# Expert stage of a two-block model: products from whole fp32 weights, one load for each expert, and blocks of 32, 64 and 128 rows in column tiles

## The reference, cut to what matters

```python
def hier_moe(h, w_group, b_group, w_expert, b_expert, w_gate, w_up, w_down):
    ...
    combine = jnp.sum(jax.nn.one_hot(global_i, N_EXPERTS, dtype=F32) * top_w[..., None], axis=1)
    out = jnp.zeros(hf.shape, F32)
    for e in range(N_EXPERTS):
        hid = jax.nn.silu(t @ w_gate[e]) * (t @ w_up[e])
        out = out + combine[:, e:e + 1] * (hid @ w_down[e]).astype(F32)
    return out.reshape(bsz, seq, d).astype(h.dtype)
```

## Time and profile before

| | us |
|---|---|
| median of 3 runs | 1953.18 |
| lowest and highest run | 1952.9 and 1956.12 |
| profiled execution, from its first to its last instruction | 1951.2 |
| first expert load issued, from the start of the span | 1359.78 |
| window 1555 to 1895: bytes moved | 415 GB/s |

### The profile page before, as it was taken

One profiled execution on the slowest core, in us unless ns is written; L12 is line 12 of the kernel. 1 busy time (PEld: TensorE's weight loads), 2 busy tenths in 40 slices (PEclk: granted clock), 3 DMA queues, 4 the chain that ended last, 5 costly groups with the idle time before them and its releaser, 6 DMA issues.

```text
span 1951.2 us, 23763 instructions
## 1 busy us (share of the span) xinstructions
PE 1847.8 (95%) x8321; PEld 1337.0 (69%) x8321; DVE 1412.4 (72%) x2128; ACT 1031.8 (53%) x1598; POOL 105.6 (5%) x98
## 2 busy tenths in 40 slices
PE   7999999999999899999999988887899999999998
PEld 6887777777888777777864545554688766556664
DVE  5988555455598855555756976434999999999995
ACT  5644555544564455554523112212888878777773
POOL 1000000000000000000003202000020100000001
PEclk9999999999999999999999999998999999999998
DMA  7544444345654444435545523231999999999994
GB/s 238 173 141 139 139 123 120 108 130 173 176 163 151 129 145 117 130 118 154 170 126 156 162 86 119 86 107 59 366 381 379 378 417 419 411 409 413 419 415 191
DMA packets 134437, 411.53 MB, mean 211 GB/s; under 512 B 16219, under 2 KB 18011, under 8 KB 107440
## 3 DMA queue, kind: packets, MB, share of 16 engines
q1 hardware_dynamic: 129200, 405.47, 59.1%
q0 software_dynamic: 5120, 4.56, 0.8%
HBM read 406.55 MB, written 12.39 MB: 215 GB/s over the span
## 4 chain that ended last, share of the span: by engine, by line
PE 64%; DVE 21%; DMA 6%; ACT 5%; issue 3%; SPq 0%; DVEq 0%; POOL 0%; ACTq 0%; POOLq 0%
PE bank L724 13%; PE bank L726 13%; PE bank L725 13%; PE bank L775 8%; DMA w_raw<-in_w_down 6%; DVE w_lo L1283 5%; PE bank L1208 3%; DVE r L1283 2%; DVE r L1289 2%; PE bank L851 2%; PE bank L692 2%; DVE y_lo L1283 2%; DVE h_lo L1283 1%; PE bank L1218 1%; PE bank L1219 1%
## 5 line engine op out<-in xcount | busy, mean ns | idle before, releaser
L1283 DVE TENSOR_TENSOR w_lo<-w_raw,w_hi 128x1024 fp32r<-128x1024 f32 x344 | 413.2, 1217 | 242.4 <-ACT w_hi L2293 223.4
L2293 ACT CAST w_hi<-w_raw 128x1024 fp32r<-128x1024 f32 x266 | 277.4, 1047 | 164.1 <-PE bank L726 157.0
L724 PE MATMUL bank<-w_hi,h_hi 128*128 128x512 f32 x800 | 327.5, 409 | 14.7 <-DVE w_lo L1283 14.7
L726 PE MATMUL bank<-w_hi,h_lo 128*128 128x512 f32 x800 | 315.4, 394 | 0.0
L725 PE MATMUL bank<-w_lo,h_hi 128*128 128x512 f32 x800 | 315.2, 394 | 0.0
L724 PEld LDWEIGHTS bank<-w_hi,h_hi 128*128 128x128 f32 x800 | 152.4, 190 | 51.2 <-issue 15.5
L726 PEld LDWEIGHTS bank<-w_hi,h_lo 128*128 128x128 f32 x800 | 152.3, 190 | 33.8
L2464 ACT ACTIVATE r<-bank,small 128x256 f32<-128x256 f32 (+1 forms) x152 | 63.9, 425 | 206.5 <-DVE small L1286 206.5
L725 PEld LDWEIGHTS bank<-w_lo,h_hi 128*128 128x128 f32 x800 | 152.9, 191 | 29.1
L775 PE MATMUL bank<-w_raw,h_all 128*128 128x512 f32 (+1 forms) x320 | 142.0, 600 | 1.1 <-DVE h_all L1283 1.1
L1283 DVE TENSOR_TENSOR w_lo<-r,w_hi 128x1024 fp32r<-128x1024 f32 x106 | 125.1, 1217 | 0.4 <-ACT w_hi L2590 0.4
(11 more groups left out here) (431 smaller groups left out, 3487.5 us busy)
## 6 DMA issues: line engine op xcount, KB each, us to landing
w_raw<-in_w_in SPq DMA_DIRECT2D x236, 512.0 KB, 3.7
r<-in_w_gate SPq DMA_DIRECT2D x70, 1024.0 KB, 7.2
w_raw<-in_w_down SPq DMA_DIRECT2D x70, 1024.0 KB, 7.8
r<-in_w_up SPq DMA_DIRECT2D x35, 1024.0 KB, 9.2
w_raw<-in_w_up SPq DMA_DIRECT2D x35, 1024.0 KB, 8.9
w_raw<-in_w_proj SPq DMA_DIRECT2D x48, 512.0 KB, 3.7
w_raw<-in_w_out SPq DMA_DIRECT2D x24, 512.0 KB, 4.0
w_raw<-in_w_mem_kv SPq DMA_DIRECT2D x8, 512.0 KB, 4.0
```

Source lines behind the costliest of these rows:

```text
L724: e.matmul(out_, sh, mh, start=first, stop=False, skip_group_check=shared)
L726: return e.matmul(out_, sl, mh, start=False, stop=last, skip_group_check=shared)
L1283: o.did(v.tensor_tensor(out_, a, b, op), sem, value)
L2293: a.copy(halves(n)[0], raw_of(n)).then_inc(w_hi, 1)
```

## The change

All of it is in the expert stage.

- **Loads.** Each expert is loaded once: 192 loads of 1 MiB instead of 210. There are 15 places of 1 MiB (`PLACES`: R7 to R10, the `w_hi/w_lo` buffers, the `h` and `y` buffers and `w_raw`). SP issues them in one plain order; load q waits until load q - 15's last use has been counted.
- **Products.** The halves are gone (`high_half`, `low_half`, `m_hi`, `m_lo`), and every product of the stage takes the whole fp32 weights: `inner` for gate and up (L1147 of the changed kernel), `outer` for down (L1164). `select` sums both halves of the rows into one `xs` in fp32.
- **Blocks.** There are still 35, in the order of `RANKS`, with full blocks spread among small ones, and the two blocks of an expert next to each other. `ROWS` is 128 for 9 blocks, 64 for 11 and 32 for 15. `WAYS` is 128/ROWS: of a 64-row block two products, of a 32-row block four, write to different partitions of one bank (`bank[r0:r0 + n]`), each with its own stationary columns: for gate and up different parts of the sum over k, which are added behind the transposes; for down different columns of the output (512 or 256 wide). The last two blocks (`FLAT`) do the down product one way, 64 rows to two banks.
- **Rows out.** ACT copies [128 x 512] or [128 x 256] to `y_out`, and `store_rows` writes 128 pieces of 2 or 1 KB through a view of `y_rows`; the indices come from a few more small operations in `starts`.
- **Order.** All eight fills come before block 0. `outer` of block x - 1 stands behind `inner` of block x.

```diff
-BLOCK_RANK = [0, 0, 1, 1, 2, 3, 4, 5, 6, 2] + list(range(7, EXP))
...
+RANKS = [0, 15, 16, 1, 17, 18, 2, 19, 20, 3, 21, 4, 22, 5, 23, 6, 24, 7, 25, 8, 26, 9, 27, 10, 28, 11, 29, 12, 13, 14, 30, 31]
+PARTS = {0: (0, P), 1: (0, P), 2: (0, P)}
+def rows_for(rank, skip):
+    most = min(S, 2 * S // (rank + 1)) - skip
+    return P // 4 if most <= P // 4 and rank < EXP - 2 and FOUR else P // 2 if most <= P // 2 else P
+ROWS = [rows_for(r, skip) for r, skip in zip(BLOCK_RANK, BLOCK_SKIP)]
+WAYS = [P // n for n in ROWS]
+FLAT = [r >= EXP - 2 for r in BLOCK_RANK]
+LOAD = [RANKS.index(r) for r in BLOCK_RANK]
...
+        PLACES = ([R[i][:, :] for i in range(7, 11)] + [spare[i][:, :] for i in (1, 2, 3, 5, 4)] + [w_raw[:, i * 2 * D:(i + 1) * 2 * D] for i in range(3)]
+                  + [spare[0][:, :], y_flat[:, :], h_flat[:, :]])
...
+                def inner(x, kind, j):
+
+                    n, ways = ROWS[x], WAYS[x]
+                    if j == 0:
+                        take(gate_up, (kind, x))
+                    bank = banks[acc[kind, x][0]]
+                    raw = landed(x, kind, j)
+                    for i in range(4):
+                        k = 4 * j + i
+                        r0 = k % ways * n
+                        done = e.matmul(bank[r0:r0 + n, :], stationary(x)[:, k, :], raw[:, i * FF:(i + 1) * FF], start=k < ways, stop=k >= KD - ways)
+                    done.then_inc(m_used, 1)
+
+                def outer(x, j):
+
+                    n, ways = ROWS[x], 1 if FLAT[x] else WAYS[x]
+                    wide = min(CH, D // ways)
+                    if j == 0:
+                        e.wait_ge(hid_done, x + 1)
+                        for i in range(2 if ways == 1 else 1):
+                            take(down, ("down", x, i))
+                    raw = landed(x, "down", j)
+                    for i in range(2):
+                        k = 2 * j + i
+                        for c in range(D // wide):
+                            bank = banks[acc["down", x, c if ways == 1 else 0][0]]
+                            r0 = 0 if ways == 1 else c * n
+                            done = e.matmul(bank[r0:r0 + n, 0:wide], hid_t[x % 2][:, k * n:(k + 1) * n], raw[:, i * D + c * wide:i * D + (c + 1) * wide],
+                                            start=k == 0, stop=k == 3)
+                    done.then_inc(m_used, 1)
...
+                for x in range(BLOCKS):
+                    if x:
+                        e.wait_ge(window_made, x)
+                    inner(x, "gate", 0)
+                    if x:
+                        turn_hidden(x - 1)
+                    inner(x, "gate", 1)
+                    inner(x, "up", 0)
+                    inner(x, "up", 1)
+                    if x:
+                        outer(x - 1, 0)
+                        outer(x - 1, 1)
...
+            for i in range(EXP):
+                x = LOAD.index(i)
+                expert = s.value_load(expert_i[0:1, x:x + 1], min_val=0, max_val=EXP - 1)
+                for n, kind in enumerate(("gate", "up", "down")):
+                    source = d["w_" + kind][bass.DynSlice(expert, 1)].rearrange("e (p k) n -> p (e k n)", p=P)
+                    for j in range(2):
+                        q = 6 * i + 2 * n + j
+                        if q >= len(PLACES):
+                            s.wait_ge(m_used, last_use[q - len(PLACES)] + 1)
+                        s.dma_start(PLACES[q % len(PLACES)], source[:, j * 2 * D:(j + 1) * 2 * D]).then_inc(in_moe[q % len(PLACES)], 16)
```

More of the change, by code:

```diff
@@ L579, in build @@
[L579 removed]
+        xs = by_k(over_tile("xs", KD * SLOTS, "r4", 0, F32)[:, :], KD)
+        windows = [by_k(over_tile(f"window{i}", KD * P, "r2", i * D, F32)[:, :], KD) for i in range(2)]
         def stationary(x):
[L582 to L588 removed]
@@ L614, in build @@
         gain_row = R[1][:, D:2 * D]
+        block_lane, block_part, block_ways = (bias_rows[1][:, i * BLOCKS:(i + 1) * BLOCKS] for i in range(3))
         block_rank, block_skip, block_last = (bias_rows[0][:, i * BLOCKS:(i + 1) * BLOCKS] for i in range(3))
@@ new lines, in moe @@
+                turn_hidden(BLOCKS - 1)
+                await_drained(("last",))
+                ends = Banks([0, 1, 7, 6])
+                for n in range(2):
+                    await_drained(("down", last_blocks[0], n))
+                    for t in range(T):
+                        _, bank = take(ends, ("end", t, n))
+                        e.matmul(bank[:, :], last_weights[:, 0, t, :], y_out[last_blocks[0] % 2][0:P // 2, n * CH:(n + 1) * CH], start=True, stop=False)
+                outer(BLOCKS - 1, 0)
@@ new lines, in moe @@
+                    if x:
+                        up_out(x - 1)
+                    if x + 1 < BLOCKS:
+                        move_window(x + 1)
+                    if x == 0:
+                        next(weighing)
+                    if x:
+                        hidden(x - 1)
+                    if x == 1:
+                        next(weighing)
+                    if x == 2:
+                        o.prev()
+                        last_rows()
+                    if x == 4:
+                        b, n, bank = await_full(("last",))
+                        o.did(v.tensor_copy(last_weights.rearrange("p w t s -> p (w t s)"), bank[0:P // 2, :]), drained[b], n)
@@ new lines, in gate_out, with hidden, rows_out @@
+            def gate_out(x):
+                b, _ = acc["gate", x]
+                a.wait_ge(m_used, step_of(x, "gate", 1) + 1)
+                a.copy(by_k(gate_rows[x % 2], 4), apart(banks[b][:, :], 4)).then_inc(drained[b], 1)
+            def hidden(x):
+                await_drained(("gate_t", x))
+                cols = slice(0, 4 * ROWS[x])
+                a.activation(gate_rows[x % 2][:, cols], gate_t[x % 2][:, cols], ACT.Silu).then_inc(silu_made, 1)
+            def rows_out(x):
+                a.wait_ge(m_used, step_of(x, "down", 1) + 1)
+                if x >= 2:
+                    a.wait_ge(scattered[x % 2], 16 * (x // 2))
+                if WAYS[x] == 1 or FLAT[x]:
+                    for n in range(2):
+                        b, _ = acc["down", x, n]
+                        a.copy(y_out[x % 2][0:ROWS[x], n * CH:(n + 1) * CH], banks[b][0:ROWS[x], :]).then_inc(drained[b], 1)
+                else:
+                    b, _ = acc["down", x, 0]
+                    a.copy(y_out[x % 2][:, 0:D // WAYS[x]], banks[b][:, 0:D // WAYS[x]]).then_inc(drained[b], 1)
@@ L2672, in moe @@
-                a.wait_ge(m_used, N_UNITS)
-                a.wait_ge(scattered[(BLOCKS - 1) % 2], 16 * ((BLOCKS - 1) // 2))
-                for n in range(2):
-                    b, _ = acc[("down", BLOCKS - 1, n)]
-                    a.copy(y_out[(BLOCKS - 1) % 2][0:P // 2, n * CH:(n + 1) * CH], banks[b][0:P // 2, :]).then_inc(drained[b], 1)
+                for q in range(SLOT_QUARTERS):
+                    for i in (0, 2):
+                        fill(q, i)
+                for x in range(BLOCKS + 1):
+                    if x >= 2:
+                        rows_out(x - 2)
+                    if x:
+                        hidden(x - 1)
+                    if x < BLOCKS:
+                        gate_out(x)
+                    if x == 0:
+                        softmax(lg)
+                        softmax(top2)
@@ L2678, in first @@
+                rows_out(BLOCKS - 1)
             def first(l):
```

442 lines of the change are left out of this document (111 added, 331 removed).

## The result

| | before | changed |
|---|---|---|
| median, us | 1954.65 (4 runs, 1952.9 to 1956.84) | 1898.38 (4 runs, 1895.66 to 1901.3) |
| profiled execution: its time, its span | | 1901.3, 1899.5 |
| first expert load issued | | 1361.50 |
| span behind that moment | 591.4 | 538.0 |

The ratio, changed by before, is 0.9706, 95% interval 0.9678 to 0.9734: faster by 56 us. Two more sets of runs of the changed kernel, beside the experiments, gave 0.972 (0.9705 to 0.9736) and 0.9704 (0.9684 to 0.9724). The prediction was 1915, 17 us more than came.

What follows compares the result with a forecast made beforehand. Most of the stage was taken to wait for weight loads; start at 1373.8, PE's pace to 1537, loads to 1885, end at 1910.5 and 3 us of clock gave a 1913.5 us span, 1915 us for the run; range 1893 to 1955.

Steps and rivals of the forecast that it cites:

- What bounds the kernel before: Expert stage before: PE sets the pace 1402 to 1538; from 1555 to 1895 it waits for weights at 415 GB/s.
- (1) The start: Start of the expert stage: first load unchanged at 1359.8, 64 fills taking 9.9 us, block 0 starting at 1373.8 instead of 1369.0.
- The price of a product: PE in the expert stage: a whole fp32 product of 512 columns takes 0.905 us, a full block 23.2 us.
- The tiles: Small blocks on PE: column tiles overlap with 5% loss for two, 20% for four; 12.9 us per 64-row block, 8.0 per 32-row.
- (2) PE sets the pace first: Early stage: loads fill 15 places and wait for PE up to load 55; PE takes 163 us, to 1537.
- (3) Then the loads: Rest of the stage behind load 55: loads at 2.53 us each set the time, ending at 1885 us.
- (4) The end: After the loads: last PE products end at 1903, then 7.6 us as before, so the span ends at 1910.5.
- (5) The clock: End of the kernel: PE may run at 1.2 instead of 2.4 GHz after waiting; 3 us taken, between 0 and 11.
- What costs nothing: Whole stage: work on DVE and ACT, some 4 us a block, scatters and SP's waits stay hidden beside PE and the loads.
- bytes are slower: Rival, loads-bound part: full blocks of fp32 products hold the DMA to 386 GB/s, 1940 us; first rival's range 1930 to 1949: 0.20.
- four tiles as good as two: Rival, 32-row blocks: four tiles take twice the ideal, 12.4 us instead of 8.0, 1949 us; within the first rival's 0.20.
- The slower case: Rival, whole stage: tiles don't overlap as they must, all blocks cost 23.2 us on PE, 2196 us; slower given 0.16.

Runs made afterwards that it cites:

- the two runs on tiles: Changed kernel with all blocks but the last two 128 rows wide: 2124.66 us; changed kernel with 32-row blocks computed as 64 rows in two tiles: 1934.62 us.

## Why the prediction was right, step by step

The direction, the mechanism and the range were right. The span came out 14 us shorter than the 1913.5 of the sum. By the steps of the prediction:

**What bounds the kernel before.** "The stage waits for bytes" behind 1555 was too strong. PE was busy 327.13 of 340 us there, and without the bytes the kernel gained only 16 us. Both bounds lay almost together, and the change had to move both; that it does was in the sum, where each has its own term. DVE, set down as lying beside the loads, was busy 306.33 of 320 us without the bytes: it had hardly room either, but did not hold PE back there.

**(1) The start.** Block 0 began at 1374.69, forecast 1373.8. The loads began 1.7 us later than before and the low quarter was ready at 1365.6 instead of 1363.9, and the 64 fills took 8.9 us, forecast 9.9.

```profile
1374.69 13.90 PE L1147 MATMUL bank<-r,xs 128*128 128x512 f32 x32
1388.42 3.60 PE L1147 MATMUL bank<-r,window 128*128 128x512 f32 x8
```

**The price of a product.** It was 5% too high. The 32 records of block 0's first sixteen products span 1374.69 to 1388.42, the start of the next group: 13.73/16 = 0.858 us. I had divided 3.62 by four, and a group's duration has the whole last record in it, of which some 0.16 us lie beside the next group. Here four products read 3.60 as a group too, and follow each other after 3.44.

**The tiles.** Right that they overlap, and the loss was mis-sized: 20% taken for four tiles and 5% for two, none measured in either. The place with two tiles in the earlier trace rows had shown no loss, and that was the better guide for four. The rule of the Trainium skill (TensorE: Matmul & The Clock Gate, Part 3) that loads of weights overlap only with another row group, as a mechanism 2196 us here, doesn't hold for these column tiles: 0.86 us for four products with four loads of weights. Nor does its 2.38 for three tiles describe four of this form, which reach 4.0.

**(2) PE sets the pace first.** By the run with quarter loads PE's work is 428 us, forecast 478. A full block took 21.7 us (forecast 23.2), a 32-row block 6.5 (8.0), a 64-row block 11.6 (12.9), one of the last two 15.1 (16.3): 9 x 1.5 + 15 x 1.5 + 9 x 1.3 + 2 x 1.2 are the 50 us. So PE let go of the pace earlier: pauses came near 1412 and 1468 as foreseen (1408, 1470), the third, near 1531, did not. By the last update of its semaphore the second load of the tenth expert, load 55, had landed at 1529.3 where the forecast has it at 1540.5. Because only the part ahead of it counts, 50 us of error in PE's work became 11 in the time. This is the term that failed, in size.

**(3) Then the loads.** The 136 loads behind load 55 landed from 1529.3 to 1877.1 (the last packet ends at 1876.5), which is 2.56 us each, forecast 2.53; the queue's bytes alone, above, gave 2.52. So 3.7 of the 11 us were lost again on the way, and that two misses pulled against each other is luck. What the forecast did not have is that a load is as late as its latest part. The 16 updates of its semaphore lie 1.0 us apart at load 55, 8.2 at load 185 and 9.2 at the last, where the first comes at 1867.9. From there the rate falls, with four gathers of rows (L2713) beside it from 1870.7 on:

```profile
1867.90:1876.50 8.60, 7.70 (x28) 2.29 (x25) 0.95 (x2) 0.58 (x1) 4.06 (x4) 1.00 0.85 327
```

How much of that the gathers add, no run tells; the last load landed 3.1 us behind the one ahead of it. By its last packet it is 8.5 us early (1876.5, forecast 1885). The Trainium skill's 358 GB/s for one core (DMA: Bandwidth & Descriptors, Specifications) is there half of what a stack gives to two cores; it is no limit for this kernel, which runs on one core and moved 415.6 GB/s of weights alone. The measurement decides, as it did before.

**(4) The end.** From the last landing to PE's last down product 15.5 us, forecast 18: the two groups of down products took 7.0 us each and not 7.5, and the four of L1204 followed without the wait of 0.7. The sum of the prediction also put the last half of `w_up` at 1880.5, where two loads ahead of 1885 is 1879.9. Behind that 7.5, forecast 7.6.

**(5) The clock.** 3 us taken, none came in this execution: here is the window of the changed kernel's end, full clock.

```profile
1822.00:1897.00 75.00, 64.64 (x252) 22.29 (x250) 19.78 (x29) 8.30 (x16) 6.97 (x7) 1.00 0.78 318
```

The clock was low all the same, at 1.2 GHz in short stretches between 1665 and 1823, where PE goes and waits for loads in turn; the window of 1757.90 to 1761.30 above is one (0.50). There the loads set the pace anyway, as the prediction had said, though no run takes the low clock away to show it. In the kernel with the moved down products the clock was low at the very end and the last four products took 4.66 instead of 3.70 us, so a term for it was right to have. The sum of the differences is 8.5 + 2.5 + 0.1 + 3 = 14.1 us, which is the 14.0 between the forecast span and the measured one; all four went the same way.

**What costs nothing** cost nothing: with PE busy 433.33 of 434 us, the run with quarter loads leaves no room for DVE, ACT, the scatters (6.5 us to land) or the waits of SP.

**The rivals.** That bytes are slower (1940) or four tiles as good as two (1949): the first fell with 421 GB/s, the second with the two runs on tiles; forced, it gives 1934.62, less than my 1949 since both of its prices were high. The slower case is real where the tiles are taken away, at 2125.

## What to carry to other kernels

Before changing what seems bound by bytes, ask how near the next bound is: here taking away three quarters of the bytes gave 16 us of 1954, and only moving both bounds gave 56. When two resources need nearly the same time in sum (428 us of PE, 484 of loads at 2.52), the order in which their uneven pieces come decides: the same pieces in order of size cost 64 us, and look in the trace for pauses of the one while the other is busy: by the packets they add up to 68 us in the order of size and to 17 in the changed kernel, which is 51 of the 64. Take the price of a pipelined instruction from the distance of two starts, not from a group's duration divided by its count.

## What the runs showed of the hardware that I had not expected

- fp32 products with 32-column weights in four column tiles ran at four times the rate of whole ones: 3.44, 1.72 and 0.86 us for four products of 512 columns in one, two and four tiles, each with its own load of weights.
- With 9 places instead of 15, and loads that land 7 to 14 us after their issue, the DMA moved 386 GB/s between 1600 and 1940 where it moved 420 with 15.
- Under a full queue the 16 semaphore updates of one load drift apart: 1.0 us at load 55, 8.2 at load 185 of the changed kernel, 12.6 at the last load where every block loads its own weights and the loads never pause. Behind the late pause of the kernel with the new order they were 2.0 apart at the last load.
- TensorE's granted clock fell to 1.2 GHz time and again where PE went and waited for loads in turn, mean 0.95 over 325 us (and 0.87 over 300 us in the order of size, where PE was idle for a third of the time), and was 1.00 over 695 us where PE never waited.
- The moment at which the stage begins moved between 1353.2 and 1365.6 us among kernels that are the same up to there, more than several of the effects looked for; the length behind it repeated to 1.3 us.
